# The head of a fused two-block kernel: rows turned token tile by token tile, and work moved between VectorE, ScalarE and GpSimd

## The reference, cut to what matters

```python
h = rms_norm(x, norm1_g)          # x * rsqrt(mean(x*x) + eps) * g, per token
p = h @ w_in                      # 1024 x (512 u, 512 v, 256 s, 2048 gates)
s_in = p[..., o_s5:o_gate]        # input of the s5 scan
uv = gelu(p[..., :o_s5])          # input of the gMLP
lam_bar = exp(lam * dt)           # s5: powers and tables come from this
b_bar = ((lam_bar - 1.0) / lam)[:, :, None] * bmat
```

## Time and profile before

| what | value |
|---|---|
| time, median of 3 runs | 2765.81 us (2765.22 to 2766.4) |
| time of the profiled execution | 2764.47 us |
| its span in the profile | 2762.7 us |
| TensorE busy | 2713.6 us (98%) |
| VectorE busy | 1795.4 us (65%) |
| ScalarE busy | 1532.3 us (55%) |
| GpSimd busy | 1033.1 us (37%) |

### The profile page before, as it was taken

The page is one execution under the profiler, slowest core; times in us unless marked ns, Lnnn a source line. Parts: engine busy times, 40 slices in busy tenths (PEclk is TensorE's granted clock), DMA queues, the critical chain, the costliest instruction groups (busy, mean ns, idle before and its releaser), DMA issues.

```text
span 2762.7 us, 35693 instructions
## 1 busy us (share of the span) xinstructions
PE 2713.6 (98%) x12846; PEld 2232.3 (81%) x12846; DVE 1795.4 (65%) x1963; ACT 1532.3 (55%) x1959; POOL 1033.1 (37%) x506
## 2 busy tenths in 40 slices
PE   7999999999999999999999999999999999999999
PEld 6887888668888888888888887997787888887787
DVE  8972113888888888888888897824554444434362
ACT  5231004367777777777777775426566544445321
POOL 0012222012222223222232232738888855554530
PEclk9999999999999999999999999999999999999999
DMA  5021114499999999999999993522222333337441
GB/s 169 26 75 39 38 54 152 176 388 402 388 383 383 382 382 381 386 383 383 383 378 385 384 346 142 184 98 99 93 107 96 116 130 125 124 124 251 137 183 61
DMA packets 168540, 615.81 MB, mean 223 GB/s; under 512 B 21185, under 2 KB 47825, under 8 KB 135409
## 3 DMA queue, kind: packets, MB, share of 16 engines
q1 hardware_dynamic: 162672, 593.23, 57.0%
q0 software_dynamic: 5328, 20.07, 2.6%
q10 hardware_dynamic: 434, 1.08, 0.1%
HBM read 551.30 MB, written 61.97 MB: 222 GB/s over the span
## 4 chain that ended last, share of the span: by engine, by line
PE 89%; DVE 8%; DMA 1%; issue 1%; ACT 1%; POOL 0%; SPq 0%; DVEq 0%; ACTq 0%
PE bank L1757 24%; PE bank L1423 19%; PE bank L1424 18%; PE bank L1425 18%; PE bank L1770 2%; PE bank L1903 1%; PE bank L1926 1%; PE bank L1893 1%; PE bank L1914 1%; PE bank L1820 1%; PE bank L1779 0%; DMA buffer<-in_wstream 0%; DVE heT_lo L3113 0%; DVE buffer L2791 0%; ACT heT_hi L2320 0%
## 5 line engine op out<-in xcount | busy, mean ns | idle before, releaser
L3063 DVE TENSOR_TENSOR slots_lo<-buffer,slots_hi 128x2048 fp32r<-128x2048 f32 x383 | 849.1, 2285 | 101.0 <-ACT slots_hi L2274 101.0
L2274 ACT ACTIVATE slots_hi<-buffer 128x2048 fp32r<-128x2048 f32 x384 | 708.6, 1950 | 40.9 <-PE bank L1757 25.4
L1307 POOL DMA_INDIRECT xacc<-buffer x15 | 276.5, 18435 | 610.5 <-ACT buffer L2342 610.5
L1348 POOL TENSOR_TENSOR w_lo_set<-buffer,w_hi 128x512 fp32r<-128x512 f32 x210 | 301.9, 1469 | 131.1 <-ACT w_hi L2406 129.4
L1757 PE MATMUL bank<-slots_hi,xsT_hi 128*128 128x512 f32 x960 | 256.9, 389 | 3.4 <-DVE xsT_lo L3081 3.4
L1757 PE MATMUL bank<-slots_lo,xsT_hi 128*128 128x512 f32 x960 | 257.4, 390 | 0.0
L1757 PE MATMUL bank<-slots_hi,xsT_lo 128*128 128x512 f32 x960 | 257.3, 390 | 0.0
L1757 PEld LDWEIGHTS bank<-slots_hi,xsT_hi 128*128 128x128 f32 x960 | 180.2, 188 | 41.3 <-issue 3.6
L1757 PEld LDWEIGHTS bank<-slots_hi,xsT_lo 128*128 128x128 f32 x960 | 180.8, 188 | 37.6
L1757 PEld LDWEIGHTS bank<-slots_lo,xsT_hi 128*128 128x128 f32 x960 | 180.6, 188 | 37.6
L1423 PE MATMUL bank<-slots_hi,heT_hi 128*128 128x512 f32 x512 | 202.5, 395 | 3.1 <-DVE heT_lo L3113 3.1
(11 more groups left out here) (538 smaller groups left out, 5599.2 us busy)
## 6 DMA issues: line engine op xcount, KB each, us to landing
buffer<-in_w_gate SPq DMA_DIRECT2D x128, 1024.0 KB, 7.9
buffer<-in_w_up SPq DMA_DIRECT2D x128, 1024.0 KB, 6.7
buffer<-in_w_down SPq DMA_DIRECT2D x128, 1024.0 KB, 8.6
buffer<-in_wstream SPq DMA_DIRECT2D x154, 512.0 KB, 4.2
gd<-buffer SPq DMA_DIRECT2D x28, 512.0 KB, 3.9
buffer<-gd SPq DMA_DIRECT2D x20, 512.0 KB, 6.5
buffer<-in_x SPq DMA_DIRECT2D x16, 512.0 KB, 8.9
od<-buffer SPq DMA_DIRECT2D x48, 130.0 KB, 2.0
```

The costliest lines, as they stand in the source:

```text
L1307: nc.gpsimd.indirect_dma_start(out=xacc, out_offset=bass.IndirectOffsetOnAxis(ap=idx_scatter, axis=0), in_=ys, in_offset=None, compute_op= ...
L1348: nc.gpsimd.tensor_tensor(lo, chunk_raw[p % 2][i], hi.bitcast(F32), ALU.subtract).then_inc(chunk_split.sem, 1)
L2274: fn(slots_hi[:, n_ % NH, :], slots[n_ % NS], ACT.Copy).then_inc(slot_high_ready, 1)
L3063: tt2(slots_lo[:, place_of(n_), :], slots[n_ % NS], slots_hi[:, n_ % NH, :].bitcast(F32), ALU.subtract).then_inc(slot_split, 1)
```

## The change

- **TensorE**: half 0 is turned by the new `turned_rows`, token tile by token tile. As soon as row tile t is scaled, its eight pieces go to the eight banks. So all banks become full during the last tile, one turn apart, where before bank 0 was full after four turns and the last bank after 32.
- **Squares**: ScalarE squares rows 0 and 2 before the first root and 4, 5 and 6 after it; VectorE squares rows 1, 3 and 7 (before, only row 3). ScalarE's square root function is loaded ahead of its first square.
- **VectorE's order**: the squares of rows 1 and 3 come before the twelve small operations 2639 to 2650, which move behind the scaling of rows 4 to 7. The scaling of rows 4 to 7 comes directly behind the second s tile's low part. `hT_low(8, 16)` and the two u tiles' low parts come before the other small operations and the powers.
- **GpSimd**: `s5bc` is issued once row 3 of x has landed, with a semaphore of its own that VectorE waits on just before the scaled B matrix. The high part of the second s tile is made when ScalarE has made four `hT_hi` pieces.

```diff
--- before.py
+++ after.py
@@ -1248,14 +1248,16 @@
                                                 ALU.subtract).then_inc(tile_split, 1)
 
             pool.dma_start(cols, a["cols"]).then_inc(consts_loaded, 16)
-            pool.dma_start(s5bc.rearrange("p a b c -> p (a b c)"), a["s5bc"]).then_inc(consts_loaded, 16)
             pool.dma_start(s5d, a["s5d"]).then_inc(consts_loaded, 16)
             pool.dma_start(small[:, 384:392], a["lncols"]).then_inc(consts_loaded, 16)
             step(nc.gpsimd.memset(ident, 0.0))
             nc.gpsimd.affine_select(out=ident, in_=ident, compare_op=ALU.not_equal, fill=1.0, base=0,
                                     pattern=[[-1, P]], channel_multiplier=1).then_inc(ident_ready, 1)
-            for i in (I_S, I_S + 1):
-                nc.gpsimd.tensor_copy(high_tile(i), wait_tile(pool, i)).then_inc(tile_high_ready, 1)
+            pool.wait_ge(x_moved[3], 16)
+            pool.dma_start(s5bc.rearrange("p a b c -> p (a b c)"), a["s5bc"]).then_inc(upb_loaded, 16)
+            nc.gpsimd.tensor_copy(high_tile(I_S), wait_tile(pool, I_S)).then_inc(tile_high_ready, 1)
+            pool.wait_ge(hT_high_ready, 4)
+            nc.gpsimd.tensor_copy(high_tile(I_S + 1), wait_tile(pool, I_S + 1)).then_inc(tile_high_ready, 1)
             b1.wait_full(pool, ("v", NT - 1))
             for dst, name in ((wsT, "wsT"), (bsB, "bsB")):
                 pool.dma_start(dst.rearrange("p a b -> p (a b)"), a[name]).then_inc(ln_there, 16)
@@ -1449,6 +1451,15 @@
             pe.wait_ge(ident_ready, 1)
             hT_parts, bra_parts = (hT_hi, hT_lo), (bra_hi, bra_lo)
 
+            def turned_rows():
+
+                for t in range(4):
+                    pe.wait_ge(xn_ready, t + 1)
+                    for k in range(KD):
+                        last = turn(b1.bank(("hT", k))[:, t * P:(t + 1) * P], x1[t][:, k * P:(k + 1) * P], ident)
+                        if t == 3:
+                            last.then_inc(full1, 1)
+
             def turned_x(first, end):
 
                 for j in range(first, end):
@@ -1476,7 +1487,7 @@
                 for h in range(2):
                     split_feature_tile(b1, ("u", 2 * f + h), w, hT_parts, h, KD)
 
-            turned_x(0, 8)
+            turned_rows()
             s_tile(0, 0)
             s_tile(1, 0)
             turned_x(8, 16)
@@ -1621,7 +1632,7 @@
                     last = turn(bank[:, t * P:(t + 1) * P], Yt[:, 4 * jq + t, fh * P:(fh + 1) * P], ident)
                 last.then_inc(full1, 1)
             gates_1("GA", 1)
-            pe.wait_ge(upb_loaded, 32)
+            pe.wait_ge(upb_loaded, 48)
             for j in range(4):
                 b1.wait_drained(pe, ("yT", j))
             for j in range(4):
@@ -2014,12 +2025,14 @@
             act.wait_ge(s5_to_act, 1)
             fn(MI[6], MI[4], ACT.Exp).then_inc(act_to_s5, 1)
             fn(MI[7], MI[4], ACT.Tanh, scale=0.5).then_inc(act_to_s5, 1)
+            first_junk = {0: junk(0), 2: at(30752, DM), 4: at(31776, DM), 5: junk(0), 6: at(30752, DM)}
+
             def first_square(tt):
 
                 act.wait_ge(x_moved[tt], 16)
-                if tt:
-                    act.wait_ge(squares_done, tt)
-                fn(junk(0), x1[tt], ACT.Square, accum_out=ssum[:, tt:tt + 1]).then_inc(squares_done, 1)
+                if tt > 4:
+                    act.wait_ge(squares_done, tt - 4)
+                fn(first_junk[tt], x1[tt], ACT.Square, accum_out=ssum[:, tt:tt + 1]).then_inc(squares_done, 1)
 
             def first_roots(h):
 
@@ -2029,11 +2042,12 @@
             act.wait_ge(s5_to_act, 2)
             fn(MI[10], MI[8], ACT.Sin).then_inc(act_to_s5, 1)
             fn(MI[11], MI[9], ACT.Sin).then_inc(act_to_s5, 1)
-            for tt in range(3):
-                first_square(tt)
             fn(MI[31], MI[3], ACT.Sqrt)
+            first_square(0)
+            first_square(2)
             first_roots(0)
-            act.wait_ge(consts_loaded, 64)
+            first_square(4)
+            act.wait_ge(consts_loaded, 48)
 
             def hT_high(first, end):
 
@@ -2058,10 +2072,10 @@
                 fn(uT[:, j // 2, (j % 2) * HALF:(j % 2 + 1) * HALF], bank[:], ACT.Gelu).then_inc(drained1["act"], 1)
 
             hT_high(0, 8)
-            for tt in range(4, NT):
-                first_square(tt)
+            first_square(5)
+            first_square(6)
+            first_roots(1)
             s_there(0, 0)
-            first_roots(1)
             tile_high(I_U)
             tile_high(I_U + 1)
             s_there(1, 0)
@@ -2142,7 +2156,7 @@
             for k in range(2):
                 act.wait_ge(brB_ready, k + 1)
                 fn(brB_hi[k], brB[:, k, :], ACT.Copy).then_inc(br_high_ready, 1)
-            act.wait_ge(upb_loaded, 32)
+            act.wait_ge(upb_loaded, 48)
             fn(upb_hi.rearrange("p a b -> p (a b)"), upb[:, 0:8].rearrange("p a b -> p (a b)"), ACT.Copy).then_inc(
                 br_high_ready, 1)
             gates_there("GB", 1)
@@ -2634,6 +2648,26 @@
                     stt(hT_lo[:, k, hs], b1.bank(("hT", j))[:], col("norm1", k), hT_hi[:, k, hs].bitcast(F32), ALU.mult,
                         ALU.subtract).then_inc(drained1["dve"], 1)
 
+            def row_squares(tt):
+
+                dve.wait_ge(x_moved[tt], 16)
+                step(stt(tA[:, 0:DM], x1[tt], 1.0, x1[tt], ALU.mult, ALU.mult, accum_out=ssum[:, tt:tt + 1]))
+
+            row_squares(1)
+            row_squares(3)
+            dve.wait_ge(squares_done, 2)
+            dve.sem_inc(squares_done, 2)
+            norm_scale(0, 0)
+            rows_normal(0)
+            tile_low(I_S)
+            dve.wait_ge(consts_loaded, 48)
+            hT_low(0, 8)
+            tile_low(I_S + 1)
+            row_squares(7)
+            dve.wait_ge(squares_done, 7)
+            dve.sem_inc(squares_done, 1)
+            norm_scale(0, 1)
+            rows_normal(1)
             dve.wait_ge(act_to_s5, 5)
             ea, th_, sh, ch = M[6], M[7], M[10], M[11]
             step(stt(M[13], sh, 2.0, ch, ALU.mult, ALU.mult))
@@ -2648,22 +2682,12 @@
             step(tt2(M[20], lim, lim, ALU.mult))
             step(tt2(M[19], M[19], M[20], ALU.add))
             step(v.reciprocal(M[19], M[19]))
-            dve.wait_ge(x_moved[3], 16)
-            step(stt(tA[:, 0:DM], x1[3], 1.0, x1[3], ALU.mult, ALU.mult, accum_out=ssum[:, 3:4]))
-            dve.wait_ge(squares_done, 3)
-            dve.sem_inc(squares_done, 1)
-            dve.wait_ge(squares_done, 4)
-            v.tensor_scalar(msq[:, 0:4], ssum[:, 0:4], 1.0 / DM, EPS, ALU.mult, ALU.add).then_inc(msq_ready, 1)
+            hT_low(8, 16)
+            tile_low(I_U)
+            tile_low(I_U + 1)
             step(tt2(M[20], M[16], lre, ALU.mult))
             step(tt2(M[21], M[18], lim, ALU.mult))
             step(tt2(M[20], M[20], M[21], ALU.add))
-            dve.wait_ge(root_ready, 1)
-            step(v.reciprocal(rinv[:, 0:4], root[:, 0:4]))
-            rows_normal(0)
-            tile_low(I_S)
-            dve.wait_ge(consts_loaded, 64)
-            hT_low(0, 8)
-            tile_low(I_S + 1)
             step(tt2(M[20], M[20], M[19], ALU.mult))
             step(tt2(M[21], M[18], lre, ALU.mult))
             step(tt2(M[22], M[16], lim, ALU.mult))
@@ -2672,8 +2696,6 @@
             step(tt2(M[23], ea, ea, ALU.mult))
             step(tt2(M[23], M[23], M[23], ALU.mult))
             step(tt2(r8, M[23], M[23], ALU.mult))
-            norm_scale(0, 1)
-            rows_normal(1)
 
             pR, pI = PW[:, 0], PW[:, 1]
             def complex_multiply(oR, oI, xR, xI, yR, yI, shape):
@@ -2705,9 +2727,7 @@
                 complex_multiply(pR[:, :, sh_], pI[:, :, sh_], pR[:, :, sl], pI[:, :, sl],
                                  over(pR[:, :, w_], w_), over(pI[:, :, w_], w_), (16, w_))
 
-            hT_low(8, 16)
-            tile_low(I_U)
-            tile_low(I_U + 1)
+            dve.wait_ge(upb_loaded, 16)
             complex_multiply(BBR, BBI, s5bc[:, 0], s5bc[:, 1], over(M[20], 16), over(M[21], 16), (16, 16))
 
             for ri in range(2):
```

## The result

The changed kernel takes 2771.26 us (median of 20 runs) where the kernel before, timed beside it, takes 2766.93 us (20 runs). The ratio is 1.0014, with a 95% interval from 1.0008 to 1.0020: some 4 us slower, between 2.2 and 5.5 us. The forecast was 2769.0 us, 3.2 us above the first three runs of the kernel before (median 2765.81). The median of all its 20 runs is 1.1 us higher, so the two shifts are what to compare: 3.2 us forecast, 4.3 us measured. The profiled execution took 2770.86 us, with a span of 2769.0 us.

A forecast was written before the change was run, and what follows sets the result against it. VectorE's unbroken string was taken to bound the head. Scaling at 12.1 plus 35.4 us puts B at 47.5 instead of 44.26, 3.2 us late: 2764.47 + 3.2 = 2767.7, plus 1.3 to the median, 2769.0 us; range 2766.3 to 2771.6.

The forecast's parts named there:

- What bounds the head: From 29 to 149 us VectorE's unbroken string of work sets when the gates begin; TensorE has 1.7 us to spare.
- Rival 1: At the kernel's start, TensorE starting 2.2 us earlier is what counts: at most 1.7 us gained, 2764.1 us; chance 0.05.
- When rows are scaled: Start of `rows_normal(0)`: 12.1 us instead of 14.30, with row 3 landing at 9.2 and GpSimd's cast delaying `msq`.
- Rival 2: At row 3's landing, moving `s5bc` brings nothing: row 3 at 10.4, scaling at 13.3, delay 4.4 us, 2770.2 us; chance 0.13.
- From the scaling to B: From `rows_normal(0)` to the scaled B matrix: 35.4 us instead of 29.96, so B starts at 47.5 instead of 44.26.
- The new wait of VectorE for the first bank: Before `hT_low(0)`, VectorE waits 2.8 us for half 0's turned bank, where before it waited 0.30 us.
- all slow: In half 0's turns, every turn at the slow pace: turn 25 starts 6.0 us after the scaling instead of 5.5.
- The second cast: GpSimd's high part of the second s tile, moved beside `hT_low`, costs nothing, as `hT_low` has one input in PSUM.
- Rival 3: In half 0's low parts, GpSimd's second cast holds `hT_low` for up to 1.04 us: 2770.0 us; chance 0.08.
- The clock: Behind TensorE's 6.5 us wait at 77.5, slow matmuls lose 1.7 us once, covered by 1.7 us to spare at 149.
- rival 4: In the s tiles TensorE runs slow, 0.14 us more per matmul: 2770.6 us with twelve, 2773 with 30; chance 0.06.
- TensorE leads everywhere and passes the delay on: Behind the merge tile's low part (149.0, now 152.2), the rest of the program keeps VectorE's 3.2 us delay.

The follow-up runs named there:

- The reversed edit: The changed kernel with the `s5bc` transfer issued first again, behind cols: 2773.54 us, ratio 1.0019 to the kernel before.
- the last four kernels: Changed with first high part by ScalarE (1.0009); changed with `s5bc` first (1.0019); before with small operations late (1.0014); changed with VectorE's string full (0.9982).
- The best version: Changed kernel with small operations and powers moved to fill VectorE's string, row 7's square and first high part on ScalarE: 2763.87 us, 0.9982 to the kernel before.

## Why the prediction was right, point by point

Right are the direction, the mechanism and the time, which lies inside the stated range. VectorE's lateness doesn't lie in the 2.3 to 4.0 us that had a chance of 0.60: it is 4.3 us, and the time (2771.26) is near the top of its range (2771.6). Two terms were mis-sized, both to the same side.

- **What bounds the head.** Right. In all ten kernels VectorE's string took 103.5 to 103.6 us from B to the merge tile's low part, and TensorE's gates followed it by 1.3 to 1.8 us. TensorE's earlier start was worth nothing: in the changed kernel and in the one with small operations late it started earlier and the head got longer. Rival 1 is out. The whole times bear it out: in eight of the nine kernels the median differs from that of the kernel before by what G does, within 1.3 us (the kernel with turns in TensorE's wait is the exception).
- **When rows are scaled.** Forecast 12.1, measured 12.61. The step that was mis-sized is the landings: row 3 came at 9.82, so 0.66 us earlier than 10.48 and not 1.28, and the first s tile behind it, with which the cast starts, at 11.07 and not at 10.4. The reversed edit gave 0.56 us for row 3. In three other kernels with a late `s5bc` row 3 was there between 9.24 and 9.86, and in the one with 9.24 the cast began at 10.49 and rows were scaled at 12.03: the forecast's own figures, so the size depends on the execution. The cast stood in the way of `msq` as foreseen, 0.90 us. Rival 2 (no gain at all) is out.
- **From the scaling to B.** Forecast 35.4, measured 35.97. The new wait of VectorE for the first bank was worked out as 2.8 us and measured as 3.5. The first bank came 7.37 us behind the scaling and not 6.7, for two reasons. Turns stayed slow for longer than granted (the first 26 at 0.213 us each; 32 took 6.37 us), so turn 25 started 6.05 us behind the scaling, which is the prediction's case "all slow". And a slip in the sum: 5.5 is where turn 25 starts, while the 0.36 us to ScalarE that were added to it count from a turn's end. ScalarE came 0.52 us behind the start. The rest of the working held: eight low parts 5.36, from row 7's square to the second scaling 2.07, the two paths that end together at half 1 (VectorE free at 33.67, ScalarE's first piece from 32.80). The two mis-sized terms, 0.5 and 0.6 us, make the forecast's 3.2 us the measured 4.3.
- **The second cast.** Free, as the Trainium skill has it (SBUF — State Buffer, section Who interferes with whom): eight low parts with one input in PSUM took 5.36 us with the cast from 21.67 on beside them, and 5.36 us without it. Rival 3 is out. What the same section says of two-port instructions agrees with the 0.90 and the 3.29 us above. It went the other way too: with small operations in the waits the cast started at 10.19, while VectorE squared row 3 from two inputs in SBUF (9.81 to 10.96), and took 1.74 us instead of 1.04.
- **The clock.** TensorE kept its level in the s tiles (rival 4 is out), and fell to 1.2 GHz in the 6.8 us wait, as the forecast had it. The loss was 2.3 to 2.5 us and not 1.7, so the 1.7 us to spare didn't cover all, and 0.5 us came on top of VectorE's 4.3 in this execution (nothing to 0.2 us in three others). The first gate matmul is 4.84 us later in all.
- **The rest of the program.** "TensorE leads everywhere and passes the delay on" holds up to 540 us (4.72 us at 500) and on the whole, but not in each execution, as the last section shows.

## What to carry to other kernels

An engine's share over the whole program hides which engine strings a stage together: take the stage's waits and find the engine that has none. To move work out of such a string's way, look where it stood: here 23 small operations stood in waits, cost nothing there, and cost 5 us in the open. A finer pipeline (by token tile) can fill its consumer's buffers later; here it made the head 1.9 us longer by itself, and 0.34 us of its wait were left once that was given other work. Whether it then beats turning by bank, no run shows.

## What was not expected of the hardware

**The spread of whole times goes with TensorE's clock behind waits, far from the change.** In the 33 runs of the kernel before that stand beside the last four kernels, the 3 runs with a mean granted clock of 0.998 took 2765.2 us in the mean and the 3 with 0.995 took 2770.7 us. Matched instruction by instruction with the profiled execution of the kernel before, the changed kernel is 4.72 us late at 500 us, 4.04 at 2500 and 6.65 at 2575. The kernel with turns in TensorE's wait is 3.95, 6.54 and 12.73 us late at the same places. Nothing of the kernels differs behind 150 us. The windows of TensorE over those two stretches, for the kernel before, then for the changed kernel and for the one with turns:

```profile
540.00:600.00 60.00, 54.65 (x174) 0.97 0.95 377
2500.00:2600.00 100.00, 91.40 (x446) 1.00 0.67 230
```

```profile
540.00:600.00 60.00, 54.81 (x163) 0.93 0.96 379
2500.00:2600.00 100.00, 91.50 (x435) 0.97 0.71 243
```

```profile
540.00:600.00 60.00, 54.48 (x151) 0.88 0.93 369
2500.00:2600.00 100.00, 89.68 (x417) 0.93 0.70 237
```

Both stretches have waits of TensorE in the same places in every kernel. In one kernel's profile the clock falls there for longer than in another's, or not at all, and such a stretch costs microseconds (between 2500 and 2575 us, 1.3 to 6.2 us against the profiled execution of the kernel before in seven kernels, and nothing in the two others), as much as the whole change. The best version's profile loses its 3.0 us in the same way (0.4 us early at 1000 us, none at 2500), so its gain rests on the 11 runs and on G. The profiled execution of the kernel before had few of them, and its 2764.47 us lie 2.5 us under that kernel's median. Why the kernel with turns is slow in all its nine runs (2773.25 to 2777.49, granted clock 0.994 to 0.996, for 0.995 to 0.998 of the kernel before beside it) stays open: its head is 3.9 us late, its median 7.7 us above the kernel before. Whether extra turns can bring that about far behind them, or those runs fell so by chance, no run here shows.

**The fall is also why the head of the changed kernel is 0.5 us later than VectorE's lateness makes it.** A wait that brings TensorE to its lower level, as the 6.8 us here did, is paid twice: once as the wait, and again by the matmuls behind it, as far as TensorE has nothing to spare.
